# One TensorE step of a chunked scan, placed behind instead of in front of the attention step beside it

## The reference, cut to what matters

```python
def hgrn_scan(k, v, log_f, s0, q=None):      # in chunks of tokens
    def step(s, inp):
        s_new = exp(last)[..., None] * s + einsum('bhsd,bhse->bhde', kc * exp(last - cum), vc)
        o_inter = einsum('bhtd,bhde->bhte', qc * exp(cum), s)
        att = einsum('bhtd,bhsd,bhtsd->bhts', qc, kc, decay)
        return s_new, o_inter + einsum('bhts,bhse->bhte', att, vc)
```

## Time and profile before

| what | value |
|---|---|
| time, median of 3 runs | 2669.34 us (2665.15 to 2670.06) |
| the profiled execution's own time | 2664.76 us |
| its span in the trace | 2662.9 us |
| TensorE busy | 2491.5 us, 94% of the span |
| VectorE, ScalarE, GpSimd busy | 33%, 29%, 30% |
| mean granted TensorE clock | 0.95 |
| memory traffic | 80 GB/s over the span |

### The profile page before, as it was taken

How to read it: one execution, slowest core, us unless ns; L and a number is a source line. 1 busy time by engine, 2 the same in 40 slices (tenths; PEclk the granted TensorE clock), 3 DMA queues, 4 the chain that set the end, 5 groups by cost and what they waited for, 6 DMA issues and landing times.

```text
span 2662.9 us, 37662 instructions
## 1 busy us (share of the span) xinstructions
PE 2491.5 (94%) x16546; PEld 1902.8 (71%) x16546; DVE 869.2 (33%) x1277; ACT 781.2 (29%) x980; POOL 794.7 (30%) x280
## 2 busy tenths in 40 slices
PE   6997889999999999979899999999799879899998
PEld 4874566777777786456788888888578336788886
DVE  3003346256256434732411111112451652311113
ACT  4322233122234323423321122122432433322222
POOL 3232233433333123402222222222221422344442
PEclk9997999999999999879999999999999778999999
DMA  4431024444443101002111111111211002222321
GB/s 175 170 135 33 17 97 156 158 182 149 175 160 127 48 9 47 3 2 95 48 64 63 64 64 64 64 51 37 89 40 42 6 2 95 79 96 97 108 88 56
DMA packets 41571, 216.66 MB, mean 81 GB/s; under 512 B 4088, under 2 KB 13064, under 8 KB 18112
## 3 DMA queue, kind: packets, MB, share of 16 engines
q1 hardware_dynamic: 38184, 207.87, 21.3%
q10 hardware_dynamic: 3224, 6.40, 0.7%
HBM read 212.12 MB, written 2.13 MB: 80 GB/s over the span
## 4 chain that ended last, share of the span: by engine, by line
PE 77%; DVE 6%; ACT 3%; issue 1%; DMA 0%; POOL 0%; DVEq 0%; ACTq 0%; POOLq 0%
PE PS L676 60%; PE PS L679 3%; PE PS L1114 2%; PE PS L1147 2%; DVE s_states L1513 2%; PE PS L762 1%; DVE a_lo L599 1%; PE PS L1710 1%; DVE tmp L606 1%; PE PS L1814 1%; PE PS L1909 1%; PE PS L1126 1%; PE PS L1164 1%; DVE x L619 1%; ACT w_hi L805 1%
## 5 line engine op out<-in xcount | busy, mean ns | idle before, releaser
L2037 POOL TENSOR_TENSOR w_lo<-raw,w_hi 128x2048 fp32r<-128x2048 f32 (+3 forms) x164 | 660.6, 4032 | 1537.8 <-ACT w_hi L805 1537.8
L676 PE MATMUL PS<-a_hi,w_hi 128*128 128x512 f32 (+1 forms) x2104 | 703.6, 376 | 49.6 <-DVE a_lo L599 25.2
L676 PE MATMUL PS<-a_lo,w_hi 128*128 128x512 f32 (+1 forms) x2104 | 687.5, 368 | 0.0
L676 PE MATMUL PS<-a_hi,w_lo 128*128 128x512 f32 (+1 forms) x2104 | 681.3, 365 | 0.0
L676 PEld LDWEIGHTS PS<-a_hi,w_hi 128*128 128x128 f32 x2104 | 363.4, 191 | 149.8 <-issue 71.9
L676 PEld LDWEIGHTS PS<-a_hi,w_lo 128*128 128x128 f32 x2104 | 365.3, 191 | 67.9
L676 PEld LDWEIGHTS PS<-a_lo,w_hi 128*128 128x128 f32 x2104 | 364.7, 191 | 62.0 <-issue 1.5
L805 ACT ACTIVATE w_hi<-raw 128x2048 fp32r<-128x2048 f32 (+2 forms) x146 | 270.4, 1852 | 398.2 <-PE PS L676 185.4
L676 PE MATMUL PS<-hid_lo,w_hi 128*128 128x512 f32 (+1 forms) x784 | 261.2, 370 | 0.0
L676 PE MATMUL PS<-hid_hi,w_hi 128*128 128x512 f32 (+1 forms) x784 | 260.8, 369 | 0.2 <-issue 0.2
L676 PE MATMUL PS<-hid_hi,w_lo 128*128 128x512 f32 (+1 forms) x784 | 258.8, 367 | 0.0
(11 more groups left out here) (220 smaller groups left out, 2437.3 us busy)
## 6 DMA issues: line engine op xcount, KB each, us to landing
raw<-in_w_ada SPq DMA_DIRECT2D x48, 1024.0 KB, 6.9
raw<-in_w_ff SPq DMA_DIRECT2D x32, 1024.0 KB, 4.8
raw<-in_w_in SPq DMA_DIRECT2D x27, 1024.0 KB, 4.8
raw<-in_w_gate SPq DMA_DIRECT2D x22, 1024.0 KB, 4.7
raw<-in_w_up SPq DMA_DIRECT2D x22, 1024.0 KB, 4.7
raw<-in_w_down SPq DMA_DIRECT2D x16, 1024.0 KB, 4.8
raw<-in_w_out SPq DMA_DIRECT2D x12, 1024.0 KB, 5.1
raw<-in_w_down SPq DMA_DIRECT2D x8, 768.0 KB, 4.3
```

The source lines that it names most:

```text
L676: mm = p.matmul(ps[:, dst], wv[:, k, idx * P:(idx + 1) * P], av[:, k, dst], start=first, stop=last)
L2037: pool.tensor_tensor(w_lo[:, m % 2, ks, 0:ncol], raw[:, i % 3, ks, 0:ncol], w_hi[:, m % 2, ks, 0:ncol].bitcast(F32), ALU.subtract).then_in ...
```

## The change

The TensorE loop of the scan yields twice per tick. Whatever a tick holds apart from k = 10 stays in front; the step k = 10 runs after the position (tick + 0.9). The loops of the other engines are as before.

```diff
             for tick in range(ticks):
                 for n in range(len(hs)):
-                    if 0 <= tick - LAG * n < SCAN_TICKS:
+                    if 0 <= tick - LAG * n < SCAN_TICKS and tick - LAG * n != 10:
                         step(n, tick - LAG * n)
+                yield (tick + 0.9) / (ticks + READ_TICKS)
+                for n in range(len(hs)):
+                    if tick - LAG * n == 10:
+                        step(n, 10)
                 yield (tick + 1) / (ticks + READ_TICKS)
```

## The result

The kernel after takes 2639.23 us (median of 4 runs, 2636.28 to 2641.79) against 2667.24 us for the kernel before on the same chips (median of 4, 2661.69 to 2670.06). The ratio is 0.9898, interval 0.9880 to 0.9916: 27 us faster, between 22 and 32. The forecast was 2652 us with a range down to 2644, so the sign was right, but the gain is 1.6 times the 17.4 us forecast and lies beyond the fast end of the range. Timed again on another chip the same kernel stood at 0.9921 (0.9899 to 0.9944), 21 us faster; 21 to 27 us is the gain to keep in mind.

What follows compares the result with a forecast made beforehand. TensorE, 94% busy, bounds the kernel, losing time waiting for VectorE's chain of states and at the low clock. Gains 11.4 + 3.2 + 2.4 + 0.4 = 17.4 us take the 2669.34 us median to 2652, range 2644 to 2661.

Steps and rivals of the forecast that it cites:

- last layer, first three halves: Attention step fills 2.81 of 5.29 us wait, plus 1.0 us of clock: 3.8 us a half, 11.4 us in all.
- last layer, last half: Eight of sixteen L1806 Fourier records fit into the 8.04 us wait for the states: 3.2 us gained, between 2 and 4.
- middle layer, last half: Eight of 20 Fourier records go into the output step's wait: 2.4 us gained, between 1.5 and 3.4.
- rest of the middle stage: First half's 0.41 us wait goes, 0.4 us gained; second and third halves merely swap TensorE work, nothing gained.
- first block: Output step changes places with attention step 13, a swap without a wait: nothing gained, stage within 1 us.
- The order and the waits: Output step trades places with one attention step per half; states end unchanged; last layer's first three waits keep 2.5 us.
- a sign of being wrong: On VectorE, L1525 and L1527 would wait over 3 us, with a TensorE wait right behind them.
- the first rival: Output comes too late for VectorE's L1525/L1527, reaching TensorE: at most 12 us against 17.4, so 2664; chance 0.08.
- The clock: Last layer's first three outputs gain 1.0 us each at full clock; the low clock behind them counts only in the range.
- The rule: Short idle times between matmul groups swing the clock, so a shorter wait saves none; the three halves stay at their floor.
- the clock falls where it held: Middle layer's second and third halves lose the clock, first half's low stretch grows: 20.7 us cost, 2676; chance 0.04.
- The slow end of the range: Whole kernel at 2661 us: the floors of the gains less one lengthened low-clock stretch, about 8 us.

Runs made afterwards that it cites:

- the filled wait: Kernel before with four pairs of useless constant products put into the wait of the last layer's first three halves, no step moved: ratio 0.9973, 7 us faster.
- the later layers: Output step moved in the middle and last layer only, first block in its old order, against the kernel before: ratio 0.9909, 24 us faster; timed again 0.9900.

## Why the prediction was right, and where it was not

The account of the profiled execution, each line against the prediction's own step:

| step | forecast | measured |
|---|---|---|
| last layer, first three halves | 11.4 | 5.4 + 4.8 + 3.3 = 13.5 |
| last layer, last half | 3.2 | 5.8 |
| rest of the last stage | 0 | 1.2 |
| middle layer, last half | 2.4 | 5.8 |
| rest of the middle stage | 0.4 | 3.9 |
| first block | 0 | -4.9 |
| outside the stages | 0 | 3.2 |
| sum | 17.4 | 28.5 |

**The order and the waits: right.** One attention step went ahead in each half, the end of the states stayed where it was, and 2.5 us of wait remained of 5.3, three times; the last halves took eight Fourier records into theirs. The idle time of the last stage fell by 11.6 us, as 3 x 2.8 + 3.3 has it. "Outputs" comes later on VectorE, as feared: in the middle layer's first half L1527 waits 3.89 us for L1710, which the prediction had called a sign of being wrong if a wait of TensorE stood right behind it. L1480 follows it without a wait of its own, and nothing on TensorE waits for either, so the first rival fell:

```profile
1088.32 1.15 DVE L1527 COPY proj<-PS 128x192 f32<-128x192 f32 x4 [3.89 <-PE PS L1710]
...
1090.39 0.90 DVE L1480 TENSOR_TENSOR s_qi<-proj,s_E 128x768 f32<-128x768 f32 x1
```

**The clock: the step that failed.** The prediction saw that "the clock depends on what surrounds the small matmuls", but priced it too low. It said of the low clock behind the output "I count no gain for it and keep it for the range", took 1.0 us a half for the output itself, 3.0 in all, and nothing in the last halves. In the profiled execution the clock was worth 8.9 us in the last stage and 8.6 in the middle one. Its own bounds broke in the two last halves: 5.8 us each, against "between 2 and 4" and "between 1.5 and 3.4". The first three halves of the last layer, 13.5 us, lie within three times 2.8 to 6.7. Measured there: behind the outputs of the first two halves the low stretch went from 11.6 to 6.2 and from 10.7 to 7.4 us, half of which is 2.7 and 1.6 us saved; in the third it grew from 6.3 to 8.0, 0.9 lost. The outputs, from L1704 to the L1114 behind, took 4.5, 4.2 and 3.9 us instead of 4.67, so 0.1, 0.5 and 0.8 saved, less than the 1.0. With the 2.8 of wait that is 5.6, 4.9 and 2.7 us, against 5.4, 4.8 and 3.3 in the lengths. In each last half the forecast missed about half of the gain: 1.9 us of the output at the full clock and 1.2 us of the Fourier records behind it stood beside the 3.3 us of wait (less 0.5 us, since the eight records in front ran slower than I had taken them, 3.75 us). A wait that is filled in front of small matmuls can be paid twice, once as idle time and once as clock: 11.6 and 8.9 us in the last stage here. Where it was only shortened the clock gave 2.4 us beside 7.6 of wait, and in three of nine traces of the last layer and three of eight of the middle one the last half got no clock for its output at all.

**The rule.** The section of the Trainium skill that the prediction named ("TensorE: Matmul & The Clock Gate", "A second HAM failure mode: psum-queue depth-cycling") says that short idle times between groups of matmuls suffice to make the clock swing. The trace agrees so far: with 2.5 us of wait left the clock fell at each of the three outputs (0.53, 0.63 and 0.68 over them). What the prediction drew from it, that no clock would be saved and each half would stay at 2.8 us, did not hold: the halves gained 5.4, 4.8 and 3.3, and the filled wait showed 0.69 us matmuls straight behind the output of the first half.

**The first block: wrong in sign.** "A swap without a wait, nothing" was true of the step that moved and not of the step that it was moved past. The output step had covered the wait for the exponentials that open a group. The trace of before could have told: at 242.57 and 341.56 us, where an attention group opens with no output step beside it, L1114 waits 1.84 us each. 1.84 us of that wait, 0.7 us more of TensorE waiting for nothing that the profile shows (1.07 against 0.35), and 6.8 us more of low clock, half of it lost, make 5.9 us; the stage is 4.9 longer, and 6 to 8 us from its updates on in the three traces. What the 0.7 us is stays open; an expectation above calls it fetch, which no view shows. The rival "the clock falls where it held" was right in kind, in another place than it named and at a sixth of its price, 3.4 us against 20.7; in the middle layer, where it was placed, the mean clock rose from 0.86 to 0.91.

The slow end of the range doesn't add up, though nothing hangs on it: the floors, 14.0 us, less a stretch that costs 8 are 6 us and 2663, not 2661.

**What is chance.** The middle stage took 198 to 205 us in traces with none or only its swaps moved, and 188.8 to 199.9 where its last half was moved; the profiled execution is the shortest of all. So of the 9.7 us there some 4 are the last half's (23.0 us on the mean of the eight executions that move it, 26.9 of the nine that don't), the swaps' part is within the spread, and so are the 3.2 us outside the stages (2122 to 2131 us over all traces). By its parts the change is worth 24 us in the later layers (14 of it in the last) less 8 in the first block, 16 us, each part known to about 5; the two direct comparisons, 21 and 27, lie above that but their intervals reach down to 15 and 22. How the middle layer's share splits stays open at this precision. On the means of the traces the last stage gives 18.9 us (14.6 forecast), the middle layer's last half 3.9 (2.4) and its swaps some 2 (0.4), and the first block takes 6.7 (0). The sum, 18 us, comes near the forecast's 17.4 by luck: the clock left out and the cover left out nearly cancel.

## What to carry to other kernels

When independent dense work can go in front of small matmuls that wait for another engine, value both what it fills and the clock that it may keep up in and behind them, and look at more than one trace, since the clock did not hold every time here; products of constants in that place are a cheap way to measure the second part alone. Before swapping two steps on an in-order engine, ask of the one that comes earlier what it will wait for: the step being moved away may be its cover, and other places of the trace where the same step stands uncovered give the price. And when a wait is left over, shorten the chain behind it before moving the waiting step further: the first gave 14 to 18 us more here, the second took the whole gain back.

## What the runs showed that I had not expected

Adding work made the kernel faster: 48 records of useless float32 matmuls, 11.1 us of TensorE time, took 7 us off the whole. And the same kernel differs by several us from one execution to the next: the middle layer's three swapped halves took 104.2 and 112.5 us in two traces of the later layers, and the last half of the last layer 17.2 and 20.3 in two of the change. The last layer's stage, by contrast, took 176.3 to 176.6 us in all four traces of kernels that leave it as it was. A single profile is good for where time goes, and here not for whether 2 or 3 us were won.
